# Turned picks and slots' weights from one product per token tile, on a two-block transformer kernel

## The reference, cut to what matters

```python
scores = jax.nn.sigmoid(jnp.dot(xt, router_w))
...
gate = gate / gate.sum(-1, keepdims=True)
combine = jnp.einsum('tk,tke->te', gate, one_hot(idx, N_EXPERTS))
out = jnp.zeros_like(xt)
for e in range(N_EXPERTS):                    # 16 experts, top 2 in one group of 4
    h = jax.nn.silu(xt @ w_gate[e]) * (xt @ w_up[e])
    out = out + combine[:, e:e + 1] * (h @ w_down[e])
```

## Time and profile before

| | us |
|---|---|
| median of 3 runs | 1422.52 (1420.93 to 1425.49) |
| the profiled execution, its own time | 1422.73 |
| its span, first to last instruction | 1420.8 |
| granted TensorE clock, mean over the span | 0.991 |

### The profile page before, as it was taken

One profiled execution on the slowest core, in us unless ns is written; L12 is line 12 of the kernel. 1 busy time (PEld: TensorE's weight loads), 2 busy tenths in 40 slices (PEclk: granted clock), 3 DMA queues, 4 the chain that ended last, 5 costly groups with the idle time before them and its releaser, 6 DMA issues.

```text
span 1420.8 us, 24216 instructions
## 1 busy us (share of the span) xinstructions
PE 1360.9 (96%) x10446; PEld 985.0 (69%) x10446; DVE 811.6 (57%) x1208; ACT 569.7 (40%) x848; POOL 61.0 (4%) x45
## 2 busy tenths in 40 slices
PE   6999999998799999999899999999999999999998
PEld 6887444342597543443599788788889979878886
DVE  4667122221657322222579887777667988768764
ACT  4553111110353210110355668644445665864342
POOL 1010000000120000000200000010000000001000
PEclk9999999999899999999999999999999999999999
DMA  9449999999367999999553445410455344532032
GB/s 384 157 149 401 421 422 422 423 423 421 144 237 298 376 423 423 423 423 423 220 195 136 134 149 178 149 63 3 148 195 192 142 134 149 177 117 95 4 119 89
DMA packets 47489, 340.24 MB, mean 239 GB/s; under 512 B 5296, under 2 KB 5296, under 8 KB 7568
## 3 DMA queue, kind: packets, MB, share of 16 engines
q1 hardware_dynamic: 45504, 328.03, 59.5%
q0 software_dynamic: 1872, 10.57, 1.9%
HBM read 337.53 MB, written 1.05 MB: 238 GB/s over the span
## 4 chain that ended last, share of the span: by engine, by line
PE 84%; DVE 8%; ACT 4%; DMA 3%; issue 2%; SPq 0%; DVEq 0%; ACTq 0%
PE bank L576 52%; PE bank L970 15%; PE bank L1012 7%; PE bank L582 2%; DMA arena<-wmoe 2%; DVE d_lo L1958 1%; PE bank L943 1%; PE bank L904 1%; PE bank L907 1%; PE bank L948 1%; ACT d_hi L1535 1%; ACT arena L1496 1%; PE bank L953 1%; PE bank L997 1%; ACT arena L1728 0%
## 5 line engine op out<-in xcount | busy, mean ns | idle before, releaser
L1958 DVE TENSOR_TENSOR d_lo<-ring,d_hi 128x2048 fp32r<-128x2048 f32 (+2 forms) x109 | 245.5, 2259 | 99.1 <-ACT d_hi L1535 98.7
L1535 ACT ACTIVATE d_hi<-ring 128x2048 fp32r<-128x2048 f32 (+2 forms) x115 | 216.2, 1886 | 129.5 <-PE bank L576 109.4
L576 PE MATMUL bank<-arena 64*64 64x64 f32 (+7 forms) x3680 | 164.7, 235 | 16.6 <-issue 5.8
L576 PE MATMUL bank<-xT_hi,d_hi 128*128 128x256 f32 x592 | 167.5, 283 | 0.2
L576 PEld LDWEIGHTS bank<-arena 64*64 64x64 f32 (+4 forms) x3680 | 142.7, 139 | 36.1 <-issue 15.1
L576 PE MATMUL bank<-xT_hi,d_lo 128*128 128x256 f32 x592 | 166.2, 281 | 0.0
L576 PE MATMUL bank<-xT_lo,d_hi 128*128 128x256 f32 x592 | 165.7, 280 | 0.0
L1496 ACT ACTIVATE arena<-bank 128x512 f32<-128x512 f32 (+4 forms) x188 | 100.3, 552 | 162.9 <-PE bank L576 128.9
L576 PE MATMUL bank<-d_hi,xT_hi 128*128 128x512 f32 (+1 forms) x400 | 158.1, 395 | 0.8 <-DVE d_lo L1958 0.5
L576 PE MATMUL bank<-d_hi,xT_lo 128*128 128x512 f32 (+1 forms) x400 | 156.6, 392 | 0.0
L576 PE MATMUL bank<-d_lo,xT_hi 128*128 128x512 f32 (+1 forms) x400 | 155.9, 390 | 0.0
(11 more groups left out here) (364 smaller groups left out, 2042.8 us busy)
## 6 DMA issues: line engine op xcount, KB each, us to landing
ring<-wmoe SPq DMA_DIRECT2D x84, 1024.0 KB, 18.1
ring<-wsecond SPq DMA_DIRECT2D x80, 1024.0 KB, 4.8
arena<-wmoe SPq DMA_DIRECT2D x72, 1024.0 KB, 16.9
ring<-wfirst SPq DMA_DIRECT2D x30, 1024.0 KB, 4.9
wide<-wmoe SPq DMA_DIRECT2D x24, 1024.0 KB, 17.5
xT_raw<-wmoe SPq DMA_DIRECT2D x12, 1024.0 KB, 18.2
rows<-lnrows POOLq DMA_DIRECT2D x4, 1024.0 KB, 10.4
ring<-wsecond SPq DMA_DIRECT2D x4, 848.0 KB, 10.3
```

Source lines behind the costliest of these rows:

```text
L576: mark(nc.tensor.matmul(o, lhsT, rhs, start=start, stop=stop, skip_group_check=loose), full)
L1535: nc.scalar.activation(high_of(u)[:, 0:width], raw[u % NRAW][:, 0:width], ACT.Copy).then_inc(sem("piece_high"), 1)
L1958: v.tensor_tensor(d_lo[u % NRAW][:, 0:width], raw[u % NRAW][:, 0:width], high_of(u)[:, 0:width], SUB).then_inc(sem("piece_low"), 1)
```

## The change

In `turn_picks`, the unit matrix and the weights' parts become one tensor `picked_by` of 192 columns: 128 of the unit matrix, then for each token tile 16 of the high and 16 of the low part. For each of the two token tiles one product of the picks with all 192 columns goes to a range of its own in bank 2 (columns 0 to 191, and 192 to 383); nothing is accumulated over the tiles. ScalarE reads the two runs of 128 columns. A slot's weight is then four values (high and low part, two tiles), at a distance of 16 and of 224 columns, and VectorE sums these in one reduction for either half of the partitions. The waits, the signals and the order of the work stay.

```diff
--- before.py
+++ after.py
@@ -28,6 +28,7 @@
 NPAIR = NE // 2
 SLOTS_OF = 64
 HALF_SLOT = SLOT // 2
+PICKED = 128 + 64
 NSLOT = 15
 NEARLY = 1
 PAIR_UNITS = 12
@@ -107,7 +108,7 @@
     f32 = mybir.dt.float32
     ALU = mybir.AluOpType
     ACT = mybir.ActivationFunctionType
-    AX = mybir.AxisListType.X
+    AX, AXES = mybir.AxisListType.X, mybir.AxisListType.XY
     MUL, ADD, SUB, MAX, MIN = ALU.mult, ALU.add, ALU.subtract, ALU.max, ALU.min
 
     ctx = ExitStack()
@@ -228,12 +229,12 @@
         S_KEY, S_CG, S_CNT = small[:, 680:712], small[:, 712:720], small[:, 720:736]
         S_LOGIT = small[:, 432:464]
 
-        ident_r = ctx.enter_context(nc.sbuf_tensor("ident_r", [P, P], f32r))[:, :]
+        picked_by = ctx.enter_context(nc.sbuf_tensor("picked_by", [P, PICKED], f32r))[:, :]
+        ident_r = picked_by[:, 0:P]
+        comb_hi, comb_lo = [v3(picked_by[:, P:PICKED], TT)[:, :, n * NE:(n + 1) * NE] for n in range(2)]
         sum_r = ctx.enter_context(nc.sbuf_tensor("sum_r", [P, 2 * P], f32r))[:, :]
         tri_r, ones_r = sum_r[:, 0:P], sum_r[:, P:2 * P]
         S_CHOSEN = reduced("chosen_r", small_at + 4 * 224, TT * NE)
-        comb_hi = ctx.enter_context(nc.sbuf_tensor("comb_hi", [P, TT * NE], f32r))[:, :]
-        comb_lo = ctx.enter_context(nc.sbuf_tensor("comb_lo", [P, TT * NE], f32r))[:, :]
         spill_info = ctx.enter_context(nc.sbuf_tensor("spill_info", [P, 2], mybir.dt.int32))[:, :]
         S_POOL = small[:, 608:610]
         S_MARK = small[:, 600:604]
@@ -919,13 +920,9 @@
                         if p > 1:
                             pe_eng.wait_ge(sem("put_taken"), taken + 4 * (p - 2) + 2)
                     for tt in range(TT):
-                        four = tt * NE + p // 2 * GS
-                        ins = nc.tensor.matmul(banks[2][:, T:T + GS], pick_r[:, tt, pair], comb_hi[:, four:four + GS], start=tt == 0, stop=False)
+                        ins = nc.tensor.matmul(banks[2][:, tt * PICKED:(tt + 1) * PICKED], pick_r[:, tt, pair], picked_by, start=True, stop=True)
                         if tt == 0:
                             carry(ins)
-                        nc.tensor.matmul(banks[2][:, T:T + GS], pick_r[:, tt, pair], comb_lo[:, four:four + GS], start=False, stop=tt == 1)
-                    for tt in range(TT):
-                        ins = nc.tensor.matmul(banks[2][:, tt * P:(tt + 1) * P], pick_r[:, tt, pair], ident_r, start=True, stop=True)
                     ins.then_inc(sem("comb_full"), 1)
 
                 def put_half(p, half, kept=False):
@@ -1639,7 +1636,7 @@
 
                     g = NPAIR * i + p
                     act_eng.wait_ge(sem("comb_full"), g + 1)
-                    nc.scalar.activation(put[p % 2], banks[2][:, 0:T], ACT.Copy).then_inc(sem("put_ready"), 1)
+                    nc.scalar.activation(v3(put[p % 2], TT), v3(banks[2][:, 0:TT * PICKED], TT)[:, :, 0:P], ACT.Copy).then_inc(sem("put_ready"), 1)
 
                 tokens(0, 0)
                 tokens(0, 2)
@@ -2218,9 +2215,9 @@
                 picks(0, 4).then_inc(sem("routed"), dve.sends(sem("routed")))
                 v.tensor_tensor(v3(S_COMB, TT), v3(S_COMB, TT), per_channel(S_RS[:, 0:TT], NE), MUL).then_inc(dve_step, dve.sends(dve_step))
                 dve_eng.wait_ge(dve.last, dve.value)
-                v.tensor_copy(comb_hi, S_COMB).then_inc(dve_step, dve.sends(dve_step))
-                dve_eng.wait_ge(dve.last, dve.value)
-                v.tensor_tensor(comb_lo, S_COMB, comb_hi, SUB).then_inc(sem("routed"), dve.sends(sem("routed")))
+                v.tensor_copy(comb_hi, v3(S_COMB, TT)).then_inc(dve_step, dve.sends(dve_step))
+                dve_eng.wait_ge(dve.last, dve.value)
+                v.tensor_tensor(comb_lo, v3(S_COMB, TT), comb_hi, SUB).then_inc(sem("routed"), dve.sends(sem("routed")))
                 picks(4, NE).then_inc(sem("routed"), dve.sends(sem("routed")))
                 v.tensor_reduce(S_MX[:, 0:1], S_CNT, AX, ADD).then_inc(dve_step, dve.sends(dve_step))
                 dve_eng.wait_ge(dve.last, dve.value)
@@ -2236,8 +2233,9 @@
 
                     dve_eng.wait_ge(sem("put_ready"), NPAIR * i + p + 1)
                     for m in range(2):
-                        own, at = slice(64 * m, 64 * m + 64), T + 2 * (p % 2) + m
-                        v.tensor_copy(S_CG[own, p:p + 1], banks[2][own, at:at + 1]).then_inc(sem("sums_ready"), 1)
+                        own, e = slice(64 * m, 64 * m + 64), 2 * p + m
+                        parts = v3(banks[2][own, 0:TT * (PICKED + 2 * NE)], TT)[:, :, P + e:P + e + NE + 1:NE]
+                        v.tensor_reduce(S_CG[own, p:p + 1], parts, AXES, ADD).then_inc(sem("sums_ready"), 1)
 
                 def add_put(p, half):
 
```

## The result

The changed kernel takes 1425.99 us (median of 20 runs, 1421.91 to 1430.22), the kernel before 1423.18 us (20 runs, 1420.93 to 1425.49). The ratio is 1.0017 [1.001, 1.0024]: slower by about 2.4 us. By the bound of 0.3% this is no change, as forecast, but the interval leaves out 1, and the median stands 0.5 us above the forecast's range. The fastest runs differ by 1.0 us, the medians by 2.8, the slowest by 4.7, so the loss differs from execution to execution. Executions in which the chip ran in its slower state are left out of all numbers. The profiled execution took 1426.02 us, its span is 1424.0 us, its mean granted clock 0.989.

What follows compares the result with a forecast made beforehand. The prediction took weight transfers, with DMA engines full, to bound the ends of both expert blocks. Its terms were 0 in the first block, 0 in the second and 0 elsewhere: 1422.5 us, range 1419.0 to 1425.5 us.

Steps and rivals of the forecast that it cites:

- One call: Turned picks, per pair and block: six products become two, saving 0.45 us a call (0.42 to 0.46), 7.2 us over 16.
- Where it lies: Eight calls a block: those before the first gate, first turn and even pairs' down worth 0; three odd pairs 1.36 us.
- Where the 1.36 us go: Ends of both expert blocks: TensorE arrives earlier but waits for weight landings, so 0; bounds 0 to 1.36 us a block.
- about 0.9: Sign in the second block: the DMA wait at unit 91 grows to about 0.9 us or spreads over units before.
- the first landings hang on the first gate: Both blocks: the first freed buffers, alone starting transfers without delay, depend on the first gate, which doesn't move; worth 0.
- a distance that shrinks by over 1 us: Sign of error: first gate to last up unit shortens by over 1 us in either block.
- VectorE and ScalarE: Readers of the picks: sum costs 0 to 0.05 us 32 times, copy nil to 0.2 us; both hidden, otherwise 5 us.
- The first: Rival, both blocks: freed buffers start transfers earlier, so 1.36 us each come through, 1419.8 us; chance 0.11.
- the second: Rival: TensorE is the bound throughout, all 16 calls count, 7.2 us saved, 1415.3 us; chance 0.04.
- The third: Rival, first block's last pair: longer waits lower the clock from unit 84 on, slower, 1448 us; chance 0.03.
- The fourth: Rival: 192-column products step at twice 0.12 us or more, saving next to nothing; 1422.5 or up to 1 us more; chance 0.02.
- No DMA is added, removed or moved.: Whole kernel: the change leaves all DMA transfers as they were, so this term is 0.

Runs made afterwards that it cites:

- run 1: The kernel before, run again unchanged: 1423.06 us, ratio 1.000.
- run 3: The changed kernel with four small products ahead of the two wide ones in every call, readers and layout as changed: 1423.94 us, 1.0002.
- Run 7: The kernel before with 192 satisfied waits (96 instructions) at TensorE's start, its work unchanged: 1426.58 us, 1.002.
- 9: The changed kernel with 32 small products a block, only in calls that hide them, making up the instruction count: 1423.1 us, 1.0003.
- 11: The changed kernel with the first two weight units of the second block issued two weight pieces later: 1423.19 us, 1.0006.
- 14: The changed kernel with the first two weight units of the second block issued two pieces later, once more: 1422.6 us, 0.9998.
- 10: The changed kernel with 128 satisfied waits (64 instructions) at TensorE's start: 1425.92 us, 1.0023.
- 13: The changed kernel with 32 small products in the hidden calls of the first block alone: 1426.03 us, 1.0023.
- run 8: The kernel before with sixteen more small products in the calls of pairs 2, 4, 6: a single execution, span 1434.4 us, +13.6.
- run 5: The changed kernel with 64 satisfied waits on TensorE behind each block of experts: 1431.85 us, 1.0066.

## Why the prediction was right, and where it was wrong

**Right.** *One call* saves nearly what was said: loads 0.11 us apart with 192 columns, 64 records fewer, 0.44 us by the wait of an even pair, and 0.40 to 0.43 where nothing hides it, 1.22 and 1.25 us a block for the 1.36 of the sum.

*Where it lies*: the even pair's down waits 0.65 us, as forecast; gate 0's load starts 0.76 us after VectorE's last copy in both kernels (145.54 less 144.78; 145.80 less 145.04).

*Where the 1.36 us go*: both blocks kept the pace of the landings (199.2 for 199.5 us, 194.2 for 194.3), the lead is taken back at named waits, and the repeat of before (run 1), 3.5 us late at the gate and on time at the end, shows the first block's bound by itself. The first wait was named at unit 84 with 1.76 us; it came as 0.26, 0.32 and 0.64 at units 79, 83 and 84, with a longer one (1.75) at the last up unit, whose forerunner didn't wait: the same sum spread, and sooner.

For the second block the prediction is at odds with itself: an arrival at 670.4 and a start at 672.19 make a wait of 1.8 us, not the "about 0.9" among its signs. Its reason that the first landings hang on the first gate isn't borne out either: in run 1 the gate moved by 3.5 us and the landings didn't. And its sign of being wrong, a distance that shrinks by over 1 us, is no test from one profile, since run 1 moved it by 3.2 and 1.3 us with nothing changed.

*VectorE and ScalarE* cost nothing: 160 and 383 ns, and run 3.

**Rivals.** The first (landings move) and the second (TensorE bound throughout) fall by the leads taken back in both blocks. The third fell in its place, PEclk 1.00 in the last pair; yet a lower clock, elsewhere, is by estimate the larger part of the loss. The fourth falls by the records.

**Wrong**: one sentence, "No DMA is added, removed or moved." It counted the program's DMAs and left out those that fetch the program. TensorE's instructions come over the same DMA engines, 16 KB at a time, and 128 instructions fewer moved those fetches. Priced at 0, the term measured 0.5 to 0.6 us of stall in both profiles of the change, and 4.2 us more at the low clock in the mean of 32 executions, worth up to 2.1 us by estimate: 2.4 us together. A single low stretch of 3.4 us costs 1.6 us in the first profile. Run 7 (fetches moved, the work as before: 1.002), 9 (count back: 1.0003) and 11 and 14 (this one stall removed: 1.0006, 0.9998) carry the cause. Runs 10 and 13 bound it: with the stall gone and half the count back the loss was 1.0023, so the cause is where the instructions stand as a whole, and the stall at 430 us is the one link of it that was followed to its end. The range missed for the same reason: it was made of the spread of the runs and the bounds of terms inside the blocks, and had no term for work between them.

**Open.** Why the kernels of runs 7, 10 and 13 lose between 930 and 966 us, and why all slower kernels spend more time at the low clock, was seen, not tested. That the clock's fall at 433 us is caused by the stall ahead of it is likely from the rows and not shown: the second profile has the stall without the fall, and its kernel's mean clock is as low. The split of the loss into stall and clock is an estimate.

## What to carry to other kernels

Where TensorE waits for landings at the end of a stage, instructions saved within it are worth nothing; see how much later than TensorE the last landings come before counting them, and repeat the profile, since the distance from the stage's first product to its last landing moved by 1.3 and 3.2 us between two executions of one kernel here. Fewer or more instructions on an engine also move its fetches: read part 3 of the page for the instruction queue, and look at what transfer has the least slack. For differences of 0.2%, lay both traces on each other product by product and seek the steps first; here the first one sat 70 us behind the edited code. And compare the mean granted clock over all executions, not in the profiled one alone.

## What the runs showed of the hardware

- The instruction fetches of 16 KB in the table above took 0.92 to 1.19 us on one DMA engine, and one that fell among queued 1 MB transfers went with a piece that landed 0.7 to 1.0 us later. The Trainium skill (Runtime: NRT & Kernel Launch, Instruction fetch mechanics) has each engine fetch its program in blocks of 16 KiB, 256 instructions, over a DMA queue of its own while it executes, and calls the crossing from block to block mostly hidden. The trace agrees with the block (88 transfers, 1.44 MB), and shows that a fetch that its own engine doesn't wait for can still delay another's data.
- VectorE's operation of 0.34 us took up to 1.65 us, and ended 0.15 or 0.16 us after GpSimd's second subtraction in all 17 profiles of this study. The Trainium skill (SBUF — State Buffer, Who interferes with whom) has the two engines share a pair of ports as an exclusive lock, the later one blocked for the whole instruction. The trace agrees: 1.59 us for 0.34.
- A product of four columns that brings its own weight load steps at 0.11 us, like one of 192. Soon behind rows of them the granted clock stood at the 1.2 GHz level for 3.4 us, a mean of 0.83 over 10 us, with TensorE busy throughout, at three places of the one execution of run 8.
- Two satisfied waits make one instruction on TensorE; at the start of the program 96 of them took about 10.3 us, 0.11 us each. Waits added behind the first block, ahead of a branch, cost 2.3 us behind it, most likely of waiting for code (run 5).
- Stretches of low clock differ between two executions of the same program: 10.2 us from 130.9 us in the repeat of before, 3.4 us from 133.5 in the first. In the mean of many executions they are a mark of the kernel all the same: 0.9903 for before, 0.9888 for the change.
